# A vector-engine sum moved out of the start of a two-block transformer kernel, and two handovers between stages in another order

## The reference

```python
c_act = jax.nn.silu(c)
mod = c_act @ w_ada[l] + b_ada[l]            # 2048 -> 3 * 2048
shift, scale, gate = jnp.split(mod, 3, axis=-1)
h = _rms(x, norm_g[l]) * (1.0 + scale[:, None, :]) + shift[:, None, :]
proj = h @ w_in[l]                           # 2048 -> 8192: attention and a gated recurrence
...
y = jnp.concatenate([att, hg], axis=-1) @ w_out[l]
x = x + gate[:, None, :] * y
```

## Time and profile before

| | |
|---|---|
| median of three executions | 2741.84 us |
| the profiled execution, and its span | 2739.56 us, 2738.2 us |
| PE busy | 2676.2 us, 98% of the span |
| DVE, ACT, POOL busy | 967.3, 1052.4, 1156.5 us |
| mean granted clock of PE | 0.992 of full speed |
| bytes by DMA | 323.27 MB, mean 118 GB/s |

### The profile page before, as it was taken

The page is one execution under the profiler, slowest core; times in us unless marked ns, Lnnn a source line. Parts: engine busy times, 40 slices in busy tenths (PEclk is TensorE's granted clock), DMA queues, the critical chain, the costliest instruction groups (busy, mean ns, idle before and its releaser), DMA issues.

```text
span 2738.2 us, 31307 instructions
## 1 busy us (share of the span) xinstructions
PE 2676.2 (98%) x12574; PEld 2152.6 (79%) x12574; DVE 967.3 (35%) x1557; ACT 1052.4 (38%) x1684; POOL 1156.5 (42%) x587
## 2 busy tenths in 40 slices
PE   6979999999999999999999999999999999999999
PEld 4558888888888888878888777777888888888787
DVE  3555744542232232134566233334232223221300
ACT  5324333334343443234443444444443434333311
POOL 0023334333434445453344444445555555555543
PEclk9989999999999999999999999999999999999999
DMA  9961222222322224432222223332233333333343
GB/s 377 372 239 65 82 76 95 85 89 89 104 100 81 89 83 141 146 112 85 85 77 81 97 92 100 101 104 98 101 106 108 112 110 115 113 114 112 137 140 110
DMA packets 102096, 323.27 MB, mean 118 GB/s; under 512 B 11328, under 2 KB 12864, under 8 KB 101440
## 3 DMA queue, kind: packets, MB, share of 16 engines
q1 hardware_dynamic: 98208, 307.64, 32.3%
q10 hardware_dynamic: 3744, 13.63, 1.3%
HBM read 304.45 MB, written 16.78 MB: 117 GB/s over the span
## 4 chain that ended last, share of the span: by engine, by line
PE 91%; DVE 4%; DMA 3%; ACT 1%; POOL 1%; issue 1%; SPq 0%; ACTq 0%; DVEq 0%
PE bank L771 27%; PE bank L773 26%; PE bank L772 26%; PE bank L892 2%; DMA TA<-in_w_ada 1%; PE bank L969 1%; DVE TA L1814 1%; PE bank L958 1%; PE bank L820 1%; PE bank L676 1%; DMA Y<-in_w_ada 1%; PE bank L952 1%; POOL wlo L2029 1%; PE bank L923 1%; PE bank L1004 1%
## 5 line engine op out<-in xcount | busy, mean ns | idle before, releaser
L2029 POOL TENSOR_TENSOR wlo<-wraw,whi 128x1024 fp32r<-128x1024 f32 (+3 forms) x430 | 992.7, 2310 | 1449.6 <-ACT whi L1073 1449.1
L771 PE MATMUL bank<-Hhi,whi 128*128 128x512 f32 x2928 | 1196.5, 409 | 7.1 <-DVE Hlo L2003 3.7
L773 PE MATMUL bank<-Hhi,wlo 128*128 128x512 f32 x2928 | 1146.0, 391 | 0.0
L772 PE MATMUL bank<-Hlo,whi 128*128 128x512 f32 x2928 | 1145.6, 391 | 0.0
L1073 ACT ACTIVATE whi<-wraw 128x1024 fp32r<-128x1024 f32 (+2 forms) x454 | 457.3, 1008 | 711.6 <-PE bank L773 688.7
L771 PEld LDWEIGHTS bank<-Hhi,whi 128*128 128x128 f32 x2928 | 551.9, 188 | 150.0 <-issue 30.0
L772 PEld LDWEIGHTS bank<-Hlo,whi 128*128 128x128 f32 x2928 | 552.4, 189 | 118.0 <-issue 10.6
L773 PEld LDWEIGHTS bank<-Hhi,wlo 128*128 128x128 f32 x2928 | 551.1, 188 | 119.2
L771 PE MATMUL bank<-Ohi,whi 128*128 128x512 f32 x320 | 128.0, 400 | 0.0
L773 PE MATMUL bank<-Ohi,wlo 128*128 128x512 f32 x320 | 124.8, 390 | 0.0
L772 PE MATMUL bank<-Olo,whi 128*128 128x512 f32 x320 | 124.7, 390 | 0.0
(11 more groups left out here) (261 smaller groups left out, 2465.8 us busy)
## 6 DMA issues: line engine op xcount, KB each, us to landing
wraw<-in_w_in SPq DMA_DIRECT2D x304, 512.0 KB, 3.2
TA<-in_w_ada SPq DMA_DIRECT2D x64, 512.0 KB, 7.9
wraw<-in_w_out SPq DMA_DIRECT2D x32, 512.0 KB, 3.2
wraw<-in_w_o SPq DMA_DIRECT2D x32, 512.0 KB, 3.2
wraw<-in_w_mem ACTq DMA_DIRECT2D x16, 512.0 KB, 7.2
Y<-in_w_ada SPq DMA_DIRECT2D x16, 512.0 KB, 7.2
first<-in_w_ada SPq DMA_DIRECT2D x16, 512.0 KB, 4.4
tmp_mgs<-TA SPq DMA_DIRECT2D x32, 256.0 KB, 2.1
```

The costliest lines, as they stand in the source:

```text
L771: e.matmul(out, hi[:, c], xhi[k], start=first and j == 0, stop=False)
L772: e.matmul(out, hi[:, c], xlo[k], start=False, stop=False)
L773: m = e.matmul(out, lo[:, c], xhi[k], start=False, stop=last and end)
L2029: e.tensor_tensor(M.wlo[b][:, 0:w], M.wraw[b][:, 0:w], M.whi[b][:, 0:w].bitcast(F32), ALU.subtract).then_inc(S.lo)
```

## The change

The gate's sums no longer have a pace of their own for each g. Both run in the slow list after the `BEGUN` tiles, one piece in each six slots (`GATE_SLOTS`), and each piece is loaded six slots ahead. With six slots for each of 16 pieces and two more, PE's sum of a g comes `GATE_STEPS` = 98 slots after the start of that g. `mem_turn` now lies between g = 0 and g = 1 and so about 100 slots later than before.

At the first handover, PE's first two parts of the second block take k in the order `LATE` (8 to 12, 14, 15, 13), and `h2(LOW)` is put into the streams after the first of these parts and no longer before the last HIGH part of `w_out`. At the second handover, `mx_early` does three tiles in each of the first two slots, then k = 6, none, and k = 7.

```diff
-GATE_PACE = ((1, 2), (12, 1))
+GATE_SLOTS = 6
-H2 = (*range(8, 13), *range(8), 13, 14, 15)
+LATE = (*range(8, 13), 14, 15, 13)
...
+GATE_STEPS = GATE_SLOTS * KT + 2
...
     for tile, bank, fours in BEGUN:
         for i in fours:
             do["ada"](i)
-        if 15 in fours:
-            do["gate_first"](0)
-            gate = do["gates"](0)
-        elif not fours and gate:
-            beat.add("slow", gate)
-            gate = None
...
-    do["gate_first"](1)
+    beat.add("slow", do["gates"](0))
     beat.add("slow", do["mem_turn"]())
     beat.add("slow", do["gates"](1))
...
-        if n == KT - 1:
-            for k in LOW:
-                do["h2"](k)
         do["part"]("y", LOW if n < KT - 1 else HIGH, bank, False, True)
...
-    for k in H2[13:]:
+    for k in LATE[5:]:
         do["h2"](k)
     second = (beat.open(), beat.open())
-    for n, ks in enumerate((HIGH, LOW)):
+    for n, ks in enumerate((LATE, LOW)):
         for bank, kind in zip(second, (("ik",), ("iq", 0))):
             do["part"]("h", ks, bank, n == 0, n == 1)
+            if n == 0 and bank == second[0]:
+                for k in LOW:
+                    do["h2"](k)
...
     def mx_early():
-        beat.add("slow", puts(*([mx(k), mx(k + 1)] for k in range(0, 8, 2))))
+        beat.add("slow", puts(map(mx, (0, 1, 2)), map(mx, (3, 4, 5)), [mx(6)], [], [mx(7)]))
...  tensor_program
-            c, end = slice(j * P, (j + 1) * P), j == len(ks) - 1
+            c, end = slice(k % 8 * P, (k % 8 + 1) * P), j == len(ks) - 1
...  vector_program, gates(g)
         for j in range(KT):
+            yield from rest(GATE_SLOTS)
...
-            if j % share == share - 1:
-                yield from rest(slots)
+        yield from rest(3)
...  sync_program
+    def gates(g):
+        places = M.gate_slot[g]
...
+        for j in range(KT):
+            if j >= len(places):
+                sp.wait_ge(S.adm, KT * g + j + 1 - len(places))
+            e.dma_start(places[j % len(places)], io["w_ada"][4 + g, j]).then_inc(S.adg[g][j % len(places)], 16)
+            yield from rest(GATE_SLOTS)
+        yield from rest(4)
```

More of the change, by code:

```diff
@@ L148 @@
 FIRST_LOADS, FIRST_RESTS = 26, 24
-def gate_steps(g):
-    slots, pieces = GATE_PACE[g]
-    return slots * KT // pieces
+GATE_STEPS = GATE_SLOTS * KT + 2
 def on_vector(k):
@@ L797, in gates @@
     def gates(g):
-        yield from rest(gate_steps(g))
+        yield from rest(GATE_STEPS)
         pe.wait_ge(S.adm, KT * (g + 1))
@@ L804, in gates @@
         free[BVV] = (S.adp, 5 + g)
+        yield
         yield
@@ L1050, in tensor_program @@
         setup=setup, mem=mem, mem_kv=lambda: rest(3), mem_turn=mem_turn, ada=ada, sums=sums, gain=nothing,
-        h_put=h_put, gate_first=nothing, gates=gates, hg=hg, attend=attend, window=window, put=put, x_load=nothing, h2=h2, index=index,
+        h_put=h_put, gates=gates, hg=hg, attend=attend, window=window, put=put, x_load=nothing, h2=h2, index=index,
         topk=lambda: rest(48), mix_load=nothing, out_load=nothing, end=nothing,
@@ L1214, in gates @@
     def gates(g):
-        return rest(gate_steps(g) + 1)
+        return rest(GATE_STEPS + 2)
     def chain(x, bias=0.0):
@@ L1425, in scalar_program @@
         setup=setup, mem=mem, mem_kv=mem_kv, mem_turn=mem_turn, ada=ada, sums=nothing, gain=nothing, h_put=h_put,
-        gate_first=nothing, gates=gates, hg=hg, attend=attend, window=window, put=put, x_load=nothing, h2=h2, index=index, topk=lambda: rest(48), mix_load=nothing,
+        gates=gates, hg=hg, attend=attend, window=window, put=put, x_load=nothing, h2=h2, index=index, topk=lambda: rest(48), mix_load=nothing,
         out_load=nothing, end=nothing, part=part, out=out, posts=dict(
@@ L1634, in gates @@
     def gates(g):
-        (slots, share), places, landed = GATE_PACE[g], M.gate_slot[g], S.adg[g]
+        places, landed = M.gate_slot[g], S.adg[g]
         for j in range(KT):
+            yield from rest(GATE_SLOTS)
             i, c = j % len(places), M.par[:, 64 + j:65 + j]
@@ L2012, in vector_program @@
         setup=setup, mem=mem, mem_kv=mem_kv, mem_turn=lambda: rest(2), ada=ada, sums=nothing, gain=gain, h_put=h_put,
-        gate_first=nothing, gates=gates, hg=hg, attend=attend, window=window, put=put, x_load=nothing, h2=h2, index=index, topk=topk, mix_load=nothing, out_load=nothing, end=nothing,
+        gates=gates, hg=hg, attend=attend, window=window, put=put, x_load=nothing, h2=h2, index=index, topk=topk, mix_load=nothing, out_load=nothing, end=nothing,
         part=part, out=out, posts=dict(
@@ L2131, in gpsimd_program @@
         setup=setup, mem=mem, mem_kv=idle(3), mem_turn=idle(2), ada=nothing, sums=nothing, gain=nothing, h_put=h_put,
-        gate_first=nothing, gates=gates, hg=idle(11), attend=attend, window=window, put=put, x_load=nothing, h2=h2, index=idle(3), topk=idle(48), mix_load=nothing, out_load=nothing, end=nothing,
+        gates=gates, hg=idle(11), attend=attend, window=window, put=put, x_load=nothing, h2=h2, index=idle(3), topk=idle(48), mix_load=nothing, out_load=nothing, end=nothing,
         part=part, out=out, posts=dict(
@@ L2168, in part @@
         beat.steps(x, ks)
-    def gate_load(g, j):
+    def gates(g):
         places = M.gate_slot[g]
-        e.dma_start(places[j % len(places)], io["w_ada"][4 + g, j]).then_inc(S.adg[g][j % len(places)], 16)
-    def gate_first(g):
         if g == 0:
@@ L2181, in gate_first @@
             sp.wait_ge(S.mask8, 1)
-        for j in range(len(M.gate_slot[g])):
-            gate_load(g, j)
-    def gates(g):
-        (slots, share), ahead = GATE_PACE[g], len(M.gate_slot[g])
-        for first in range(0, KT, share):
-            yield from rest(slots)
-            for j in range(first, first + share):
-                if j + ahead < KT:
-                    sp.wait_ge(S.adm, KT * g + j + 1)
-                    gate_load(g, j + ahead)
-        yield
+        for j in range(KT):
[4 more added lines that the diff above has]
+        yield from rest(4)
     def strip(which, h):
@@ L2280, in sync_program @@
         setup=setup, mem=mem, mem_kv=idle(3), mem_turn=idle(2), ada=nothing, sums=nothing, gain=nothing, h_put=nothing,
-        gate_first=gate_first, gates=gates, hg=hg, attend=attend, window=window,
+        gates=gates, hg=hg, attend=attend, window=window,
         put=nothing, x_load=x_load, h2=nothing, index=idle(3), topk=idle(48), mix_load=mix_load, out_load=out_load,
```

## The result

The changed kernel takes 2709.59 us, the median of four executions (2707.96 to 2713.21). The kernel before takes 2742.59 us beside it (four executions, 2738.43 to 2743.58). The ratio is 0.9884, 95% interval 0.9867 to 0.9901: 33 us, or 1.2%, faster, and 3.4 us under the predicted 2713. The profiled execution took 2707.96 us, its span is 2706.6 us, against 2739.56 and 2738.2.

The account below looks back on a forecast made before the run. PE, busy 98% of the span, was taken as the bound, so only its waits and the slower clock after them counted. 20.7 - 1.7 + 5.4 + 3.9 = 28.3 us gave 2713 us; own range 2708 to 2717, wider 2706.5 to 2725.

Parts of the forecast that it names:

- Part 1: Gate sums of g = 0: PE's stall at L802 goes, 22.4 us less 1.7 for its matmuls, net gain 20.7.
- Part 2: Recurrence: 8 more gate pieces on DVE there, at 0.2 us each on average, cost 1.7 us.
- The bound of +1.9: Recurrence, best case: 1.9 us gained if the two old collisions go and no new one comes.
- Rival A: Recurrence takes more back: 8 added pieces cost 7.6 us, 2719 us in all, or 2729 at 17.4; chance 0.11.
- Part 3: First handover: LOW's Hlo move behind x1 of tile 13; 5.7 us lost before, gain 5.4.
- Part 4: Second handover: L1615 no longer stands behind two Hlo on DVE; gain 3.9 us, bounds 0 and 3.9.
- rival B: Handovers don't pay, the next late thing replaces what was removed: 2718 us, or 2723 with no gain there; chance 0.10.
- C: Slower than before: SP stands at a gate load, weight buffers run dry, DVE's lateness reaches PE; 2757 us; chance 0.03.
- D: The gate stall moves to the first recurrence steps or the weights, for half of it: 2723 us; chance 0.04.

Follow-up runs that it names:

- the kernel without pieces: Changed kernel with 30 of the 32 gate pieces summed over only 2 of 1024 columns, loads and order kept: 2709.44 us.
- the halves: Changed kernel with each weight rest on POOL, from item 24 on, made in two instructions of half the columns: 2699.6 us, ratio to before 0.9845.
- the other places: Changed kernel with second-handover tiles at 0, 1, 2; 3, 4; 5; none; 6, 7, and k = 14 on POOL, not DVE: 2707.75 us.
- the one without the pieces of g = 1: Kernel before with 15 of the 16 gate pieces of g = 1 summed over only 2 of 1024 columns: 2737.84 us, ratio 0.9980.

## Why the prediction came out as it did

**Part 1, right.** 22.4 us predicted gross, 22.4 measured, alike in all ten traces with the gate's change. Both numbers rest on one trace of the stall, which is up to 2.1 us longer in others. L794 of g = 0 costs 1.8 us at its new place, for the 1.7 predicted. No weight came late.

**Part 2, wrong in sign: the step that failed.** I took -1.7 us for the recurrence, with bounds from +1.9 to -7.6; it is +3.5. The step was "a piece costs 0.2 us on average, and 8 more cost 1.7 us". It multiplied a number of pieces by an average, where the cost hangs on the place: zero at the places after (the kernel without pieces is as long), 4.1 us in all at the old ones. The bound of +1.9 was too near as well, for two reasons. It counted only the two old pieces that stand behind an L1660, and missed the one at 272.71, behind a COPY_PREDICATED, which cost two waits as well. And it took listed waits for the whole cost: the three pieces were followed by 2.4 us of listed waits and cost 4.1 us. With the halves 12 waits of 0.43 us and one of 0.85 go, 6.0 us in all, and 9.2 us are gained: a listed wait of 0.43 us stands for 0.67 of lost time. That 3.5 us came back and not 4.1 agrees with one wait of 0.43 us more, at 398.15, which the changed kernel has with and without pieces. Rival A's argument (DVE's steps are what PE waits for) was true and pointed the wrong way: PE waits for them because POOL holds them, and the old pieces pushed them into POOL's instructions.

**Part 3, right.** 5.4 us predicted, 5.2 measured by the edit alone and in the changed kernel. Of the edit's two halves only the move of LOW's Hlo counts; the order of 13, 14 and 15 doesn't.

**Part 4, mechanism partly right, size wrong.** 3.9 us predicted, 1.8 measured. I looked only at what stood ahead of L1615. Moving k = 5 ahead of L1594 was written down as if it were free, but four Hlo beside POOL take 7.61 us there, and PE waits 0.86 us for that bank; this is rival B at the one joint. With three Hlo there and the other places behind them, the predicted 3.9 is reached (4.0). There is a second share, which the order alone doesn't decide: of the 3.9 us that the kernel before lost, 1.6 were a lower clock (below), which other kernels with the same gap didn't lose. Against those the edit as made gained 0.1 to 0.2 us, and the other places 2.3 to 2.4.

**The sum.** 22.4 - 1.8 + 3.5 + 5.2 + 1.8 = 31.1 us against 28.3 predicted. Errors of +5.2 and -2.1 us partly cancel, and the predicted time of 2713 was 3.4 us too high. That it came so near is in part luck: the recurrence, with the wrong sign, more than made up for what the second handover lacked. Rivals C and D didn't happen: weights appear in no wait of PE after 185 us.

## What to carry to other kernels

An extra instruction on an engine with idle time costs by its place, and a count times an average says little: look at what runs right behind it, and whether that is then held by another engine. Where DVE and POOL work side by side and PE waits for short DVE steps, cut POOL's long instructions: a DVE step then waits for half as long. Two halves took POOL 0.1 to 0.3 us more than the whole, and PE waited for them only between the handovers, 1.5 us in all. The cut was worth 10 us here, a third of the whole change. When a wait is removed by moving work forward, go through every release that the moved work now stands ahead of, and not only the one that was late.

## What was not expected of the hardware

**A listed wait of 0.43 us costs PE 0.67 us.** In the changed kernel the last matmul before such a wait starts at 355.39 and the first behind it at 356.21, so 0.59 us more than the usual 0.23 pass. The group of eight matmuls lasts 1.13 us and not the 1.05 of an unheld one: 0.59 + 0.08 = 0.67, which is 0.24 more than listed. Twelve of 0.67 and one of 0.85 + 0.24 make 9.1 us, an estimate, where the halves gained 9.2.

**The same gap, with and without a lower clock behind it.** PE waits 2.14 us at the old second handover in the kernel before and in the one with the gate's change alone. Windows of 10 us around the gap, of the kernel before and then of the other:

```profile
2555.00:2560.00 5.00, 2.86 (x13) 2.10 (x12) 4.96 (x5) 3.61 (x7) 4.74 (x3) 1.00 0.37 134
2560.00:2565.00 5.00, 5.00 (x17) 3.90 (x16) 4.97 (x6) 0.45 (x1) 3.15 (x2) 0.66 0.14 50
```

```profile
2535.00:2540.00 5.00, 2.86 (x13) 2.05 (x13) 4.97 (x4) 3.71 (x6) 5.00 (x3) 1.00 0.36 125
2540.00:2545.00 5.00, 5.00 (x24) 4.12 (x23) 4.97 (x6) 0.27 (x2) 2.78 (x2) 1.00 0.20 52
```

In the first the granted clock is 0.66 of full speed for five us and PE runs 17 matmuls; in the second it stays at 1.00 (2.4 GHz) and PE runs 24. Of four profiled kernels with that order, two lost the 1.6 us and two didn't. PE's busy time in the window of the gap is the same in both shown (2.86 us), and the gap is 2.14 us in all four. So the loss isn't fixed by the length of the gap; what decides stays open. The Trainium skill (page "TensorE: Matmul & The Clock Gate", section "What's actually happening") says that the chip's measure of activity runs freely and isn't tied to the start of a kernel. By that rule the same gap can cost the 1.6 us in one execution and not in the next; two traces with and two without agree with it and don't prove it. The first handover of before shows the like, a spread of 1.3 us among four kernels with the same order: over the 10 us from 1201 on the granted clock is 0.95 and 0.71 in the two halves in the kernel before, 0.75 and 0.57 in the one without the pieces of g = 1, and 1.00 at the same place in the other two. So a part of what such a gap costs belongs to the run, and a gain of 1 to 2 us at one can't be put down to an edit from one profile.
